# Softmax shares in a latent-attention kernel: GpSimd weights the exponentials of three heads, TensorE spreads the shares of the fourth

## The chip, the cores and the metric

One core of a Trainium2 chip runs the whole kernel. The metric is device time in microseconds, the median of three runs. The engines of a core run their own instruction streams and meet at semaphores: TensorE (PE; its weight loads are listed as PEld), VectorE (DVE), ScalarE (ACT), GpSimd (POOL) and SyncE (SP, which only issues transfers here).

## The reference

One encoder layer over two sequences of 1024 and 512 tokens (1536 together, 12 tiles of 128): RMSNorm, a combined input projection, three mixers side by side (latent attention with 4 heads, centred pooling, gated linear attention), SiLU gates, an output projection, a residual add and a last RMSNorm. The change lies in the attention:

```python
s = (einsum('bqhd,bkhd->bhqk', qn, k_nope) + einsum('bqhr,bkr->bhqk', qr, k_rope))
p = softmax(s * MLA_SCALE, axis=-1)
return einsum('bhqk,bkhd->bqhd', p, v)        # v = latent @ w_v, per head
```

Everything is float32. The softmax is exp(s - max) divided by the row's sum; the inverse of that sum is called the share of a query here. The product with the keys' values is taken in two stages: the probabilities times the latent tokens (128 wide), and that times the head's w_v.

## The kernel before, in words

The program has three phases in order of time: a front phase (norm, input projection, pooling, linear attention; to about 410 us), the attention phase `phase_mla_attend` (about 413 to 632 us), and the output phase. Almost all float32 products are made as three products of split halves (`product`, L76 to L80: hi*hi, hi*lo, lo*hi).

The attention phase runs 48 steps, 12 query tiles for each of 4 heads. `QUERY_TILES` gives for a step the tile and the number of key tiles, `count`: 8 for the first eight tiles of a head (the long sequence: 1024 keys, wide steps) and 4 for the last four (512 keys, narrow steps). Each engine has its own loop over the step number m, and the order inside a step is written out by hand with lags. For step m:

- PE: `scores(m)` into PSUM banks 2*(m%2) and the next; in some steps `project`; in odd steps `values(p)` of the pair of tiles p=(m-4)//2; `turn(m-2)`, which transposes the exponentials of step m-2 tile by tile, in float32 against the identity (L1894); in even steps `output(p)`, p=(m-5)//2.
- DVE: the row maximum (L1821) and from it the bias -max*scale (L1824) of step m; in odd steps the gather of an earlier pair (L1829, L1831) and the low half of the latent product (L1837); the share of step m-2, a reciprocal of `total` (L1843); the low halves of the turned exponentials (L1848).
- ACT: the exponentials of step m with their row sum in `total` (L1763), written to `weights`, a ring of 3 slots; the high halves of the turned exponentials (L1777) and of the latent product (L1791).
- POOL has nothing to do in the first three heads. Its queue holds the split of the output weights `w_out` (L1712, L1717), which waits for their load, and the gates of the first output tile.

The exponentials are transposed and multiplied unnormalised, so the shares come in at the end of each pair of query tiles: a share is one number per partition (query), but the product of `output` has the queries along the free axis. Two transposes of `share[:, i].broadcast_to([P, P])` against the identity (L1914) therefore spread the 2*128 shares over all partitions, into the second half of the PSUM bank of the pair. DVE copies them to `share_row` (L1829), since it takes one operand from PSUM, and multiplies (L1831) into `keep.mixed`.

Waits that matter: `scores(m)` waits for the exponentials of m-2 (`exp_done`); the exponentials of m wait for the transposes of m-3 (`turned`); `turn(m)` waits for `exp_done`; `values(p)` waits for the gather of p-2; `output(p)` waits for `share_ready` and `latent_lo_ready`.

Of the kernel before, what the change touches and what calls it, by code (L numbers as in the profile page):

```python
# [17 lines left out]
ALU = mybir.AluOpType  # L18
# [3 lines left out]
P = 128  # L22
# [3 lines left out]
TILES = NT // P  # L26
# [15 lines left out]
HEADS = 4  # L42
# [1517 lines left out]
SLOTS = 3  # L1560
PAIR = 2 * P
PAIRS = STEPS // 2

TURN_LAG, VALUES_LAG, OUTPUT_LAG, GATHER_LAG = 2, 4, 5, 6
PROJECT_AT = {5: 0, 7: 1, 9: 2}
MIX_GATES_STEP, HEADS_GATES_STEP = STEPS - 6, STEPS - 4
SPLIT_FIRST_STEP = STEPS - 3
# [40 lines left out]
def phase_mla_attend(nc, cx, block, front, rope_dram, gates_dram, mix_dram, w_out_dram, w_out_loaded, gate_loaded, mix_loaded, psum,  # L1608
# [6 lines left out]
    with ExitStack() as mem:  # L1615
# [26 lines left out]
        latent_lo_ready = sem("a_latent_lo_ready")  # L1642
        output_done = sem("a_output_done")
        share_copied = sem("a_share_copied")
        gathered = sem("a_gathered")
        w_hi_set = sem("a_w_hi_set")
        w_split = sem("a_w_split")
# [42 lines left out]
        @block.gpsimd  # L1690
        def _(pool):
            mix, of_heads = keep.mix_first[:, :, :], keep.mixed[:, :, 0:P]
            heads_gates, mix_gates = keep.gate_first[:, 0:4, :], keep.gate_first[:, 4:KT, :]

            def multiply(out, gates):
                return nc.gpsimd.tensor_tensor(out, out, gates, ALU.mult)

            for k in range(KT):
                if k == 6:
                    pool.wait_ge(gate_loaded, 16)  # L1700
                    pool.wait_ge(mix_loaded, 16)
                    multiply(mix, mix_gates).then_inc(first_step, 1)
                if k == 7:
                    pool.wait_ge(gate_turned, 1)
                    nc.gpsimd.tensor_scalar(mix_gates, mix_gates, 1.0, 0.5, ALU.add, ALU.mult).then_inc(first_step, 1)
                    pool.wait_ge(first_step, 2)
                    multiply(mix, mix_gates).then_inc(first_step, 1)
                pool.wait_ge(w_out_loaded[k], 16)
                if k == 5:
                    pool.wait_ge(scores_done, TILES * (HEADS - 1))  # L1710
                for half in range(2):
                    nc.gpsimd.tensor_copy(keep.w_out_hi[k][half][:, :], keep.w_out[k][:, half * BLK:(half + 1) * BLK])\  # L1712
                      .then_inc(w_hi_set, 1)
                for half in range(2):
                    cols = slice(half * BLK, (half + 1) * BLK)
                    pool.wait_ge(w_hi_set, 2 * k + half + 1)
                    nc.gpsimd.tensor_tensor(keep.w_out_lo[k][:, cols], keep.w_out[k][:, cols],  # L1717
                                            keep.w_out_hi[k][half][:, :].bitcast(F32), ALU.subtract).then_inc(w_split, 1)
            pool.wait_ge(gathered, 3 * TILES // 2 + 1)
            multiply(of_heads, heads_gates).then_inc(first_step, 1)  # L1720
            pool.wait_ge(gate_opened, 1)
            nc.gpsimd.tensor_scalar(heads_gates, heads_gates, 1.0, 0.5, ALU.add, ALU.mult).then_inc(first_step, 1)
            pool.wait_ge(first_step, 5)
            multiply(of_heads, heads_gates).then_inc(gated, 2)
# [80 lines left out]
        def _(dve):  # L1805
# [10 lines left out]
            for m in range(STEPS + GATHER_LAG):  # L1816
                if m < STEPS:
# [5 lines left out]
                    dve.wait_ge(top_ready, m + 1)  # L1823
                    nc.vector.tensor_scalar(bias[:, m:m + 1], top[:, m:m + 1], keep.q_scale[:, tile:tile + 1], -1.0,  # L1824
                                            ALU.mult, ALU.mult).then_inc(bias_ready, 1)
                for p in pair_at(m, GATHER_LAG):
                    h, t = p // (2 * TB), (p % (2 * TB)) * PAIR
                    dve.wait_ge(output_done, p + 1)
                    nc.vector.tensor_copy(share_row[:, p % 2, :], psum[:, 6 + p % 2, PAIR:]).then_inc(share_copied, 1)  # L1829
                    dve.wait_ge(share_copied, p + 1)  # L1830
                    nc.vector.tensor_tensor(keep.mixed[:, h, t:t + PAIR], psum[:, 6 + p % 2, :PAIR],  # L1831
                                            share_row[:, p % 2, :], ALU.mult).then_inc(gathered, 1)
                for h, b in projected_at(m):
# [5 lines left out]
                      .then_inc(latent_lo_ready, 1)  # L1839
                if 0 <= m - TURN_LAG < STEPS:  # L1840
                    tile = m - TURN_LAG
                    dve.wait_ge(exp_done, tile + 1)
                    nc.vector.reciprocal(share[:, tile:tile + 1], total[:, tile:tile + 1]).then_inc(share_ready, 1)  # L1843
                    for n, item in turned_banks(tile):
                        dve.wait_ge(turned_hi_ready, item)
                        at = (slice(None), (tile // 2) % 2, slice(4 * n, 4 * n + 4),
# [13 lines left out]
        def _(pe):  # L1860
# [26 lines left out]
                mm.then_inc(scores_done, 1)  # L1887

            def turn(m):
                pe.wait_ge(exp_done, m + 1)  # L1890
                for n, item in turned_banks(m):
                    pe.wait_ge(turned_lo_ready, item - 2)
                    for k in range(4):
# [14 lines left out]

            def output(p):
                h = p // (2 * TB)  # L1910
                pe.wait_ge(share_ready, 2 * p + 2)
                pe.wait_ge(latent_lo_ready, p + 1)
                for n in range(2):
                    nc.tensor.transpose(psum[:, 6 + p % 2, PAIR + n * P:PAIR + (n + 1) * P],  # L1914
                                        share[:, 2 * p + n:2 * p + n + 1].broadcast_to([P, P]), ident[:, :])
                product(nc, psum[:, 6 + p % 2, :PAIR], keep.w_v_hi[:, h * P:(h + 1) * P], keep.w_v_lo[:, h * P:(h + 1) * P],
                        latent_hi[:, p % 2, :], latent_lo[:, p % 2, :]).then_inc(output_done, 1)

# [405 lines left out]
```

## Time and profile before

| | us |
|---|---|
| median of 3 runs (768.06 to 768.74) | 768.07 |
| profiled execution, its own time | 769.48 |
| span of the profile, first to last instruction | 767.7 |
| PE busy over the span | 749.1 (98%) |
| DVE busy | 410.0 (53%) |
| ACT busy | 308.3 (40%) |
| POOL busy | 221.4 (29%) |

The own time holds 1.8 us that lie outside the span. The profiled execution is 1.41 us longer than the median. Matmuls are pipelined: the duration in a matmul's row overlaps its neighbours', so what one costs PE is the distance from its start to the next start.

### The profile page before, as it was taken

To read this page: it belongs to the slowest core of one execution; us is meant where nothing else is said; L and a number is where in the kernel's file an instruction comes from. 1 tells how busy PE (TensorE), PEld (TensorE's weight loads), DVE (VectorE), ACT (ScalarE), POOL (GpSimd) and SP (SyncE) were. 2 spreads that over 40 slices of the span, in tenths; PEclk is the share of its full clock that TensorE was granted. 3 is DMA by queue.
4 is the path that set the end of the run, shared out by engine and by line. 5 is a ranking of instruction groups with operands and counts; after the bars stand their busy time and mean duration, and the time that the engine had idled before them with its cause. 6 is when DMAs were issued, how large, how long until landed. Compare 5 with 4: busy or idle time off the path is not lost.

```text
span 767.7 us, 14603 instructions
## 1 busy us (share of the span) xinstructions
PE 749.1 (98%) x6044; PEld 630.0 (82%) x6044; DVE 410.0 (53%) x733; ACT 308.3 (40%) x533; POOL 221.4 (29%) x261
## 2 busy tenths in 40 slices
PE   6999999999999999999999999999999999999996
PEld 4997867877888888888887888888888987888885
DVE  3662795366557643106164776767667664443332
ACT  5552624513434432232313645555445643323221
POOL 4123214536556631123500000000009904323320
PEclk9899999999999999999999999999999999999999
DMA  7312022001211222430124000000034025654541
GB/s 259 134 60 75 29 67 82 29 3 43 71 68 46 85 86 96 152 96 28 48 110 165 15 16 28 9 21 14 15 91 185 1 74 160 220 183 136 160 150 55
DMA packets 40188, 64.53 MB, mean 84 GB/s; under 512 B 4256, under 2 KB 23104, under 8 KB 40128
## 3 DMA queue, kind: packets, MB, share of 16 engines
q1 hardware_dynamic: 33984, 49.51, 20.0%
q10 hardware_dynamic: 6144, 14.16, 4.8%
q8 instruction: 45, 0.74, 0.4%
q14 instruction: 15, 0.12, 0.0%
HBM read 44.00 MB, written 19.27 MB: 82 GB/s over the span
## 4 chain that ended last, share of the span: by engine, by line
PE 88%; DVE 5%; DMA 2%; ACT 2%; issue 1%; SPq 1%; POOL 1%; DVEq 0%; POOLq 0%; ACTq 0%
PE psum L78 23%; PE psum L80 22%; PE psum L79 22%; PE psum L1894 5%; PE psum L1885 2%; PE psum L1886 2%; PE psum L1280 2%; PE psum L1174 1%; DMA o_gate_second<-gates_scratch 1%; PE psum L1310 1%; PE psum L1335 1%; DMA n_x_in<-in_x_dram 1%; PE psum L1204 1%; PE psum L1235 1%; PE psum L1914 1%
## 5 line engine op out<-in xcount | busy, mean ns | idle before, releaser
L78 PE MATMUL psum<-h_hi,z_w_hi 128*128 128x512 f32 (+1 forms) x480 | 184.8, 385 | 0.0
L80 PE MATMUL psum<-h_hi,z_w_lo 128*128 128x512 f32 (+1 forms) x480 | 177.8, 370 | 0.0
L79 PE MATMUL psum<-h_lo,z_w_hi 128*128 128x512 f32 (+1 forms) x480 | 177.7, 370 | 0.0
L78 PEld LDWEIGHTS psum<-h_hi,z_w_hi 128*128 128x128 f32 x480 | 91.4, 190 | 18.4 <-issue 2.2
L80 PEld LDWEIGHTS psum<-h_hi,z_w_lo 128*128 128x128 f32 x480 | 91.3, 190 | 15.8
L79 PEld LDWEIGHTS psum<-h_lo,z_w_hi 128*128 128x128 f32 x480 | 91.5, 191 | 14.2 <-issue 0.7
L78 PE MATMUL psum<-o_w_hi,o_m_hi 128*128 128x512 f32 x184 | 72.8, 396 | 0.8 <-DVE o_m_lo L2127 0.7
L80 PE MATMUL psum<-o_w_hi,o_m_lo 128*128 128x512 f32 x184 | 72.3, 393 | 0.0
L79 PE MATMUL psum<-o_w_lo,o_m_hi 128*128 128x512 f32 x184 | 72.2, 392 | 0.0
L1763 ACT ACTIVATE a_weights<-psum,a_bias,mla_q_scale 128x1024 f32<-128x1024 f32 (+1 forms) x48 | 51.2, 1066 | 47.2 <-DVE a_bias L1824 47.0
L769 POOL TENSOR_TENSOR z_w_lo<-z_w_raw,z_w_hi 128x1024 fp32r<-128x1024 f32 x17 | 42.1, 2478 | 95.3 <-ACT z_w_hi L473 95.3
L1712 POOL CAST o_w_hi<-o_w_raw 128x512 fp32r<-128x512 f32 x16 | 9.4, 620 | 196.5 <-DMA o_w_raw<-in_w_out_dram 196.5
L1821 DVE TENSOR_REDUCE a_top<-psum 128x1 f32<-128x1024 f32 (+1 forms) x48 | 50.1, 1043 | 27.7 <-PE psum L1886 27.7
L1777 ACT ACTIVATE a_turned_hi<-psum 128x512 fp32r<-128x512 f32 x80 | 44.3, 597 | 33.7 <-PE psum L1894 32.8
L1848 DVE TENSOR_TENSOR a_turned_lo<-psum,a_turned_hi 128x512 fp32r<-128x512 f32 x80 | 51.9, 683 | 2.7 <-ACT a_turned_hi L1777 2.7
L1033 DVE COPY_PREDICATED g_attn<-g_level_mask,psum 128x256 f32<-128x256 int32 x72 | 32.4, 450 | 38.8 <-ACT g_attn L644 36.7
L80 PE MATMUL psum<-a_turned_hi,mla_tokens_lo 128*128 128x256 f32 x160 | 45.3, 283 | 0.0
L79 PE MATMUL psum<-a_turned_lo,mla_tokens_hi 128*128 128x256 f32 x160 | 45.3, 283 | 0.0
L78 PE MATMUL psum<-a_turned_hi,mla_tokens_hi 128*128 128x256 f32 x160 | 45.1, 282 | 0.0
L2138 DVE TENSOR_TENSOR o_y<-psum,o_x_in 128x512 f32<-128x512 f32 x24 | 16.4, 689 | 52.4 <-PE psum L80 52.4
L1894 PE MATMUL psum<-ident,a_weights 128*128 128x128 f32 x320 | 43.6, 275 | 0.0
L486 ACT ACTIVATE z_gate<-psum 128x512 f32<-128x512 f32 x24 | 14.3, 598 | 71.6 <-PE psum L80 71.6
(236 smaller groups left out, 1446.3 us busy)
## 6 DMA issues: line engine op xcount, KB each, us to landing
z_w_raw<-in_w_z_dram SPq DMA_DIRECT2D x17, 512.0 KB, 3.4
n_x_in<-in_x_dram SPq DMA_DIRECT2D x12, 512.0 KB, 4.0
gates_scratch<-z_gate ACTq DMA_DIRECT2D x24, 256.0 KB, 2.0
o_x_in<-in_x_dram SPq DMA_DIRECT2D x12, 512.0 KB, 3.6
out_dram<-o_y ACTq DMA_DIRECT2D x11, 512.0 KB, 3.1
o_w_raw<-in_w_out_dram SPq DMA_DIRECT2D x8, 512.0 KB, 9.3
rope_scratch<-p_rope_split SPq DMA_DIRECT2D x12, 256.0 KB, 2.3
a_q_rope<-rope_scratch SPq DMA_DIRECT2D x48, 64.0 KB, 1.9
```

What stands on the lines that cost most here:

```text
L78: nc.tensor.matmul(out, a_hi, b_hi, start=first, stop=False)
L79: nc.tensor.matmul(out, a_hi, b_lo, start=False, stop=False)
L80: return nc.tensor.matmul(out, a_lo, b_hi, start=False, stop=last)
L769: nc.gpsimd.tensor_tensor(w_lo[:, o % 2, :], raw_of(o)[:, :], w_hi[:, o % 2, :].bitcast(F32), ALU.subtract).then_inc(w_lo_ready, 1)
L1033: nc.vector.copy_predicated(attn[:, t % 2, :, :], level_mask[:, n, :].bitcast(mybir.dt.int32).unsqueeze(1).broadcast_to([P, HEADS, CHUNK]) ...
L1280: mm = nc.tensor.matmul(psum[CHUNK * half:CHUNK * (half + 1), 2 + head, n * CHUNK:(n + 1) * CHUNK], keys, moving, start=True, stop=True, s ...
L1763: nc.scalar.activation(weights[:, m % SLOTS, 0:count * P].rearrange("p (a k) -> p a k", k=BLK), psum[:, banks, :], ACT.Exp, bias=bias[:, m ...
L1777: nc.scalar.activation(turned_hi[:, p % 2, 4 * n:4 * n + 4, (tile % 2) * P:(tile % 2 + 1) * P], psum[:, 4 + item % 2, :].rearrange("p (k q ...
L1821: nc.vector.tensor_reduce(top[:, m:m + 1], psum[:, banks, :], mybir.AxisListType.XY, ALU.max)\
L1848: nc.vector.tensor_tensor(turned_lo[at], psum[:, 4 + item % 2, :].rearrange("p (k q) -> p k q", k=4), turned_hi[at].bitcast(F32), ALU.subt ...
L1894: mm = nc.tensor.transpose(psum[:, 4 + item % 2, k * P:(k + 1) * P], weights[:, m % SLOTS, (4 * n + k) * P:(4 * n + k + 1) * P], ident[:, :])
L2138: nc.vector.tensor_tensor(y[:, s, cols], psum[:, 1 - s + 2 * half, :], x_in[:, s, cols], ALU.add)\
```

## The change

For the 36 steps of heads 0 to 2 (`WEIGHTED_STEPS`), POOL multiplies the exponentials in place by the share (a `tensor_scalar` with one scalar per partition, 128x1024 in wide and 128x512 in narrow steps) and signals the new semaphore `weighted`, for which `turn(m)` waits in place of `exp_done`. These 36 instructions stand ahead of everything else in POOL's queue of this phase. DVE takes the reciprocal of step m-1 right behind the bias of step m, in place of that of step m-2 later in the step. `output` no longer issues its two share transposes for the 18 pairs of these heads and doesn't wait for `share_ready`; DVE's gather of these pairs is one copy from PSUM to `keep.mixed`. Head 3 works as before.

```diff
--- before.py
+++ after.py
@@ -1562,6 +1562,7 @@
 PAIRS = STEPS // 2
 
 TURN_LAG, VALUES_LAG, OUTPUT_LAG, GATHER_LAG = 2, 4, 5, 6
+WEIGHTED_STEPS = TILES * (HEADS - 1)
 PROJECT_AT = {5: 0, 7: 1, 9: 2}
 MIX_GATES_STEP, HEADS_GATES_STEP = STEPS - 6, STEPS - 4
 SPLIT_FIRST_STEP = STEPS - 3
@@ -1642,6 +1643,7 @@
         latent_lo_ready = sem("a_latent_lo_ready")
         output_done = sem("a_output_done")
         share_copied = sem("a_share_copied")
+        weighted = sem("a_weighted")
         gathered = sem("a_gathered")
         w_hi_set = sem("a_w_hi_set")
         w_split = sem("a_w_split")
@@ -1694,6 +1696,12 @@
 
             def multiply(out, gates):
                 return nc.gpsimd.tensor_tensor(out, out, gates, ALU.mult)
+
+            for m in range(WEIGHTED_STEPS):
+                count = QUERY_TILES[m % TILES][2]
+                pool.wait_ge(share_ready, m + 1)
+                nc.gpsimd.tensor_scalar(weights[:, m % SLOTS, 0:count * P], weights[:, m % SLOTS, 0:count * P],
+                                        share[:, m:m + 1], None, ALU.mult).then_inc(weighted, 1)
 
             for k in range(KT):
                 if k == 6:
@@ -1823,11 +1831,17 @@
                     dve.wait_ge(top_ready, m + 1)
                     nc.vector.tensor_scalar(bias[:, m:m + 1], top[:, m:m + 1], keep.q_scale[:, tile:tile + 1], -1.0,
                                             ALU.mult, ALU.mult).then_inc(bias_ready, 1)
+                if 0 < m <= WEIGHTED_STEPS:
+                    dve.wait_ge(exp_done, m)
+                    nc.vector.reciprocal(share[:, m - 1:m], total[:, m - 1:m]).then_inc(share_ready, 1)
                 for p in pair_at(m, GATHER_LAG):
                     h, t = p // (2 * TB), (p % (2 * TB)) * PAIR
                     dve.wait_ge(output_done, p + 1)
+                    if 2 * p < WEIGHTED_STEPS:
+                        nc.vector.tensor_copy(keep.mixed[:, h, t:t + PAIR], psum[:, 6 + p % 2, :PAIR]).then_inc(gathered, 1)
+                        continue
                     nc.vector.tensor_copy(share_row[:, p % 2, :], psum[:, 6 + p % 2, PAIR:]).then_inc(share_copied, 1)
-                    dve.wait_ge(share_copied, p + 1)
+                    dve.wait_ge(share_copied, p - WEIGHTED_STEPS // 2 + 1)
                     nc.vector.tensor_tensor(keep.mixed[:, h, t:t + PAIR], psum[:, 6 + p % 2, :PAIR],
                                             share_row[:, p % 2, :], ALU.mult).then_inc(gathered, 1)
                 for h, b in projected_at(m):
@@ -1839,8 +1853,9 @@
                       .then_inc(latent_lo_ready, 1)
                 if 0 <= m - TURN_LAG < STEPS:
                     tile = m - TURN_LAG
-                    dve.wait_ge(exp_done, tile + 1)
-                    nc.vector.reciprocal(share[:, tile:tile + 1], total[:, tile:tile + 1]).then_inc(share_ready, 1)
+                    if tile >= WEIGHTED_STEPS:
+                        dve.wait_ge(exp_done, tile + 1)
+                        nc.vector.reciprocal(share[:, tile:tile + 1], total[:, tile:tile + 1]).then_inc(share_ready, 1)
                     for n, item in turned_banks(tile):
                         dve.wait_ge(turned_hi_ready, item)
                         at = (slice(None), (tile // 2) % 2, slice(4 * n, 4 * n + 4),
@@ -1887,7 +1902,10 @@
                 mm.then_inc(scores_done, 1)
 
             def turn(m):
-                pe.wait_ge(exp_done, m + 1)
+                if m < WEIGHTED_STEPS:
+                    pe.wait_ge(weighted, m + 1)
+                else:
+                    pe.wait_ge(exp_done, m + 1)
                 for n, item in turned_banks(m):
                     pe.wait_ge(turned_lo_ready, item - 2)
                     for k in range(4):
@@ -1908,11 +1926,12 @@
 
             def output(p):
                 h = p // (2 * TB)
-                pe.wait_ge(share_ready, 2 * p + 2)
                 pe.wait_ge(latent_lo_ready, p + 1)
-                for n in range(2):
-                    nc.tensor.transpose(psum[:, 6 + p % 2, PAIR + n * P:PAIR + (n + 1) * P],
-                                        share[:, 2 * p + n:2 * p + n + 1].broadcast_to([P, P]), ident[:, :])
+                if 2 * p >= WEIGHTED_STEPS:
+                    pe.wait_ge(share_ready, 2 * p + 2)
+                    for n in range(2):
+                        nc.tensor.transpose(psum[:, 6 + p % 2, PAIR + n * P:PAIR + (n + 1) * P],
+                                            share[:, 2 * p + n:2 * p + n + 1].broadcast_to([P, P]), ident[:, :])
                 product(nc, psum[:, 6 + p % 2, :PAIR], keep.w_v_hi[:, h * P:(h + 1) * P], keep.w_v_lo[:, h * P:(h + 1) * P],
                         latent_hi[:, p % 2, :], latent_lo[:, p % 2, :]).then_inc(output_done, 1)
```

## Rows read from the trace of the kernel before

**Rows 1.** Page, part 1: busy us, share of the span, instructions.
```profile
PE 749.1 (98%) x6044; PEld 630.0 (82%) x6044; DVE 410.0 (53%) x733; ACT 308.3 (40%) x533; POOL 221.4 (29%) x261
```

**Rows 2.** Windows: length, busy us of PE, PEld, DVE, ACT, POOL, clock, DMA.
```profile
413.00:422.00 9.00, 8.08 (x39) 6.46 (x39) 4.22 (x6) 2.91 (x6) 0.00 (x0) 1.00 0.11 31
422.00:575.00 153.00, 153.00 (x984) 136.19 (x983) 105.72 (x219) 80.48 (x153) 0.00 (x0) 1.00 0.09 25
575.00:632.00 57.00, 56.85 (x379) 50.94 (x378) 39.44 (x85) 31.19 (x58) 35.32 (x38) 1.00 0.22 84
```

**Rows 3.** Chain that ended last, 422 to 575 us, its shares by line.
```profile
by line: PE psum L78 21.3%; PE psum L79 21.3%; PE psum L80 21.2%; PE psum L1894 17.2%; PE psum L1885 8.4%; PE psum L1886 8.4%; PE psum L1914 2.3%
```

**Rows 4.** Timeline of PE: start us, us, engine, line, op, shape, count.
```profile
465.45 0.38 PE L1914 MATMUL psum<-ident,a_share 128*128 128x128 f32 x2
465.79 0.28 PE L79 MATMUL psum<-a_latent_lo,mla_w_v_hi 128*128 128x256 f32 x1
465.91 0.29 PE L80 MATMUL psum<-a_latent_hi,mla_w_v_lo 128*128 128x256 f32 x1
...
469.73 0.60 PE L1894 MATMUL psum<-ident,a_weights 128*128 128x128 f32 x4
470.40 0.39 PE L79 MATMUL psum<-mla_ckv_lo,a_q_hi 128*128 128x512 f32 x1
470.63 0.39 PE L80 MATMUL psum<-mla_ckv_hi,a_q_lo 128*128 128x512 f32 x1
```

**Rows 5.** Groups of POOL by shape: count, busy us, mean ns of one, idle before.
```profile
L769 POOL TENSOR_TENSOR z_w_lo<-z_w_raw,z_w_hi 128x1024 fp32r<-128x1024 f32 x17 | 42.1, 2478 | 95.3 <-ACT z_w_hi L473 95.3
...
L769 POOL TENSOR_TENSOR z_w_lo<-z_w_raw_second,z_w_hi 128x1024 fp32r<-128x1024 f32 x1 | 3.4, 3412 | 0.1
...
L827 POOL COPY z_window_sums<-z 128x1024 f32<-128x1024 f32 x2 | 2.1, 1042 | 2.7 <-ACT z L511 2.7
...
L827 POOL COPY z_window_sums<-z 128x512 f32<-128x512 f32 x2 | 1.2, 618 | 0.0
L1705 POOL TENSOR_SCALAR o_gate_first<-o_gate_first 128x512 f32<-128x512 f32 x1 | 0.6, 636 | 0.0
```

**Rows 6.** Timeline of all engines: steps 0 and 1, and the bias of step 13.
```profile
418.49 0.19 ACT L1763 ACTIVATION_READ_ACCUMULATOR a_weights<-psum,a_bias,mla_q_scale 128x1 f32 x1
...
419.31 0.21 DVE L1824 TENSOR_SCALAR a_bias<-a_top,mla_q_scale 128x1 f32<-128x1 f32 x1
...
422.60 0.21 DVE L1824 TENSOR_SCALAR a_bias<-a_top,mla_q_scale 128x1 f32<-128x1 f32 x1
...
422.73 0.15 DVE L1843 RECIPROCAL a_share<-a_total 128x1 f32<-128x1 f32 x1
...
469.76 0.21 DVE L1824 TENSOR_SCALAR a_bias<-a_top,mla_q_scale 128x1 f32<-128x1 f32 x1
```

**Rows 7.** Timeline of PE's weight loads: the transposes of steps 0, 1 and 12.
```profile
420.92 1.02 PEld L1894 LDWEIGHTS psum<-ident,a_weights 128*128 128x128 f32 x8
...
424.08 1.03 PEld L1894 LDWEIGHTS psum<-ident,a_weights 128*128 128x128 f32 x8
...
472.25 1.02 PEld L1894 LDWEIGHTS psum<-ident,a_weights 128*128 128x128 f32 x8
```

**Rows 8.** Timeline of all engines: one signal from POOL to ACT.
```profile
609.40 1.31 POOL L1696 TENSOR_TENSOR mla_mixed<-mla_mixed,o_gate_first 128x512 f32<-128x512 f32 x1
...
610.75 0.63 ACT L1736 ACTIVATE o_gate_first<-o_gate_first 128x512 f32<-128x512 f32 x1 [0.48 <-POOL mla_mixed L1696]
```

**Rows 9.** One line's instructions: ns min/median/max, first and last start.
```profile
L1824 DVE TENSOR_SCALAR a_bias<-a_top,mla_q_scale x48: 213/214/217, 417.1 to 618.6; 128x1 f32<-128x1 f32 x48
```

**Rows 10.** Timelines of POOL and of PE: first weight split, first product that needs the splits.
```profile
577.22 1.17 POOL L1712 CAST o_w_hi<-o_w_raw 128x512 fp32r<-128x512 f32 x2 [196.51 <-DMA o_w_raw<-in_w_out_dram]
...
622.26 0.40 PE L78 MATMUL psum<-o_w_hi,o_first_hi 128*128 128x512 f32 x1
```

## The prediction

> **What bounds the kernel now.** I read the page first: PE is busy for 98% of the span and no other engine for more than 53% [rows 1]. An average over stages doesn't say what limits the attention phase, so I went on to the windows of that phase. Its start (413 to 422 us) has about 1 us in which PE is idle. From 422 to 575 us, which is nearly all of the first three heads, PE is busy for 153.00 of 153.00 us at a granted clock of 1.00, the upper level (2.4 GHz); DVE is busy for 106 us, ACT for 80 and POOL for none [rows 2]. A busy PE need not be the cause, so the third view is the chain of waits of the same stretch: it consists of PE lines alone. No step of it goes to DVE, ACT or a transfer, and the share transposes of L1914 hold 2.3% of it [rows 3]. So in these heads an instruction taken from PE shortens the time by what PE spends on it, as long as nothing else becomes late; and the one thing that the change puts in front of PE is POOL's multiplication.
>
> **What goes away on PE.** The duration in a matmul's row (0.27 us for one share transpose) is not its price, since matmuls overlap. The distance of starts is. From the first share transpose of a pair to the second product of `output` it is 465.79 - 465.45 = 0.34 us; a product of 256 columns takes 0.12 us from start to start (465.91 - 465.79), so the two transposes hold 0.22 us, 0.11 each [rows 4]. One could fear that the first product behind a transpose is slow for another reason, and that this stays. Where four transposes are followed by a 512-column product with no share between them, the distance to the second product is 470.40 - 469.73 = 0.67 us = 4 x 0.11 + 0.23, and 0.23 is what such a product takes anyway (470.63 - 470.40) [rows 4]. So there is no such penalty. The chain gives the same by another way: 2.3% of 153 us is 3.5 us over the 16 pairs whose `output` lies in that window, 0.22 us a pair; its rounding (2.25 to 2.35%) makes 0.215 to 0.225 [rows 3]. The change removes the transposes of 18 pairs: 18 x 0.22 = 3.96 us, with 3.87 and 4.05 as ends. Their weight loads and one wait per pair go with them and are in the distances.
>
> **What is added on POOL, and when it has to be done.** No row shows a `tensor_scalar` of 128x1024 with a scalar per partition. From below: the copy of that shape takes 1.04 us [rows 5]. The nearest row is a `tensor_scalar` with constants of 128x512 at 0.64 us, close to the copy of its shape at 0.62; add the copies' difference (1.04 - 0.62) for twice the columns and it is 1.06 us [rows 5]. From above: the two-input subtractions of 128x1024 take 2.48 us, and the dearest of them took 3.41 [rows 5]. One tensor is read, as in the copy, so I take 1.06 us, and keep 1.04 and 3.41 as ends.
>
> The Trainium skill speaks against such work on GpSimd: GPSIMD Engine Reference, section 3.1 (Elementwise — side-by-side cycle accounting), gives about 2.6 cycles per element and section 4.1 sends elementwise work on a tile to VectorE. By that figure a wide multiplication would be 1024 x 2.6 / 1.2 GHz = 2.2 us, an estimate from that page. Section 3.1 ties that figure to two-input work and section 4.1 names about line rate for one input; the trace's copy and two-input rows agree with both.
>
> When must it be done? The reciprocal now stands behind the next step's bias. In the rows a reciprocal starts 0.13 us after the start of the bias in front of it and takes 0.15, so the share is there 0.28 us after that start [rows 6]. A signal from POOL to another engine took 0.04 us (609.40 + 1.31 to 610.75) [rows 8]; I take 0.04 for DVE to POOL and for POOL to PE. With w for the multiplication, the weighted exponentials of step m are there at bias(m+1) + 0.36 + w. They are due when PE loads the first of them for its transposes. Step 0: 420.92 - 419.31 = 1.61 us, so w may be 1.25. Step 1: 424.08 - 422.60 = 1.48, so w may be 1.12; step 2 is like step 1 within 0.01. Step 12: 472.25 - 469.76 = 2.49, so w may be 2.13; step 24 is like it [rows 6, 7]. Gone through in the same way, the other 31 steps allow more than 2.7. The first three steps are tight because no `values` stands between their scores and their transposes; steps 12 and 24 because the `values` and the transposes in between are those of narrow tiles.
>
> With w = 1.06 nothing waits: the tightest step keeps 0.06 us. For w = 1.25, a wide step at twice the narrow row, steps 1 and 2 wait 0.13 us once. I put 0.1 us down for this. For larger w the stalls are 2w - 2.38 us in the first three steps together (the delay of step 0 moves the scores and the bias of step 3, behind which the share of step 2 is made; that of step 1 doesn't), plus 2(w - 2.13) in steps 12 and 24 from w = 2.13, and from about 2.8 on something in other steps, which I leave out.
>
> **What is moved, and what stays hidden.** On PE, `output` and the next step's scores stand behind the wait in `turn`; they are late by the stalls just given and by nothing else. On DVE, the earlier reciprocal now waits for the exponentials of m-1 ahead of the gather and the low halves. In step 1, the tightest, that wait is over at 418.49 + 0.19 = 418.68, ahead of the bias at 419.31 [rows 6]. The share's copy and multiplication become one copy, so DVE gets back one instruction a pair; it had 47 us idle in the 153 [rows 2], and nothing in the chain waits for it [rows 3], so I count zero. POOL working beside DVE could slow it: the bias took 213 to 217 ns in all 48 steps, also in head 3 where POOL is busy for 35 of 57 us [rows 2, 9], so zero. POOL's queue: the split of `w_out`, which began at 577.22 when its load landed [rows 10], now stands behind the 36th multiplication, that of step 35, and may begin later. The splits ended before POOL's next instruction at 609.40 and are needed at 622.26 [rows 8, 10]: 12.9 us of cover, and only what is late beyond these would cost. SP's transfers wait for the same events as before and move with them.
>
> **The sum.** Against the profiled execution's own time: 769.48 - 3.96 + 0.1 = 765.6 us. That execution is 1.41 us over the median of the runs; taken off, 764.2 us, 0.5% faster.
>
> **The rivals.**
> 1. POOL's multiplication costs as much as a two-input one, 2.48 us. Then the first three steps stall 2 x 2.48 - 2.38 = 2.58 us and steps 12 and 24 together 0.70, 3.28 in all, and 0.7 us is left: 767.4, no difference that can be told. For: no row has a scalar per partition, and POOL's rows differ fourfold for other operations. Against: copy and `tensor_scalar` of 128x512 are equal within 3%. The skill's page named above has the rule for this rival, with its 2.2 us.
> 2. Slower. POOL's multiplication takes 3.41 us, as its dearest row of this size. The stalls are 2 x 3.41 - 2.38 = 4.44 us in the first three steps and 2 x 1.28 = 2.56 in steps 12 and 24, 7.0 at least, so 768.07 - 3.96 + 7.0 = 771.1. From w = 2.65 the stalls (4w - 6.64) eat the whole gain, and from 3.02 the kernel is slower by more than 0.2%. For: it is POOL's own time, once, in this trace. Against: once in 18, and for two inputs.
> 3. The change does nothing: something other than PE sets the pace of the heads, and PE's 0.22 us a pair become idle time; 768.1. For: ACT and DVE work in turns with PE in every step. Against: PE has no idle time at all in 153 us, and the chain has no other engine [rows 2, 3].
>
> **How the numbers follow.** 0.2% of the time, 1.5 us, is about what a measurement of this kernel can tell from no change. The forecast (w up to 1.3, 764.0 to 764.5) has a chance of 0.72; a w between 1.3 and 2.26, where 1.5 us or more of the gain is left (up to 766.5), 0.12; rival 1 with its surroundings 0.08, rival 3 0.03, rival 2 0.05. So faster 0.84, no difference 0.11, slower 0.05. The low end is the largest gain (4.05 us, no stall: 764.0) less 0.3 for the runs' own spread; the high end is the edge of the second case: 763.7 to 766.5.
>
> **What would show it right or wrong.** Right: L1914 has 12 instructions instead of 48; the new POOL line has 24 wide ones near 1.06 us and 12 narrow near 0.64; PE is again busy without a gap from 422 us on, and the transposes of steps 0 to 2 wait for POOL by 0.1 us at most; a head takes 6 x 0.22 = 1.3 us less. Wrong: waits of PE for POOL in steps 0 to 2, 12 and 24 (then w is over 2.1); longer DVE rows beside POOL's; gaps of PE in the middle of a head; or `w_out` splits that end close to their first product.

## The result and the profile after

The change made the kernel slower, by about as little as can be told from no change: 770.17 us (median of 20 runs) against 769.05 for the kernel before beside it, a ratio of 1.0018 with a 95% interval of 1.001 to 1.0027, so 0.8 to 2.1 us. The forecast was 3.9 us less.

The profiled execution after took 771.27 us, its span is 769.5. The page's part 1 answers to [rows 1]: PE has less to do, as intended, and POOL 87 us more.

```profile
PE 746.5 (97%) x6008; PEld 625.8 (81%) x6008; DVE 402.9 (52%) x715; ACT 307.7 (40%) x533; POOL 308.4 (40%) x297
```

The windows by stage, to be held against [rows 2] (columns as there). Of the 153 us from 422 to 575, where PE had no idle time before, it now idles for 2.95, and before 422 for 0.7 us more than it did:

```profile
413.00:422.00 9.00, 7.36 (x30) 5.47 (x30) 4.03 (x7) 3.11 (x5) 2.04 (x1) 1.00 0.13 37
422.00:575.00 153.00, 150.05 (x950) 132.16 (x951) 98.45 (x201) 79.46 (x151) 83.52 (x35) 1.00 0.08 21
575.00:632.00 57.00, 56.94 (x380) 51.00 (x379) 38.90 (x83) 31.81 (x59) 36.89 (x39) 1.00 0.23 88
```

The chain of the same stretch answers to [rows 3]. The 2.3% of the share transposes are gone, and POOL's multiplication has come into it with 7.5%:

```profile
by line: PE psum L78 19.5%; PE psum L80 19.5%; PE psum L79 19.5%; PE psum L1912 17.0%; PE psum L1901 7.5%; PE psum L1900 7.5%; POOL a_weights L1703 7.5%; DVE a_top L1829 2.4%; DVE a_bias L1832 0.4%; issue 0.4%; DVE a_share L1836 0.2%
```

The reason stands in the groups of POOL by shape. A wide multiplication took 2.85 us and a narrow one 1.57, where the forecast had 1.06 and 0.64:

```profile
L1703 POOL TENSOR_SCALAR a_weights<-a_weights,a_share 128x1024 f32<-128x1024 f32 x24 | 68.4, 2849 | 82.1 <-DVE a_share L1836 82.1
L1703 POOL TENSOR_SCALAR a_weights<-a_weights,a_share 128x512 f32<-128x512 f32 x12 | 18.8, 1568 | 27.9 <-DVE a_share L1836 27.9
```

PE's weight loads that waited for POOL, from the timeline (answers to [rows 7]; in brackets the idle time and what ended it). These seven are all: the transposes of steps 0 to 2, 12, 14, 24 and 26. Five of them the forecast had named as the tightest; steps 14 and 26 it had not (see e4_covered):

```profile
422.86 0.86 PEld L1912 LDWEIGHTS psum<-ident,a_weights 128*128 128x128 f32 x8 [1.71 <-POOL a_weights L1703]
426.16 0.86 PEld L1912 LDWEIGHTS psum<-ident,a_weights 128*128 128x128 f32 x8 [0.32 <-POOL a_weights L1703]
430.83 0.85 PEld L1912 LDWEIGHTS psum<-ident,a_weights 128*128 128x128 f32 x8 [1.70 <-POOL a_weights L1703]
...
475.65 0.86 PEld L1912 LDWEIGHTS psum<-ident,a_weights 128*128 128x128 f32 x8 [0.83 <-POOL a_weights L1703]
483.97 0.86 PEld L1912 LDWEIGHTS psum<-ident,a_weights 128*128 128x128 f32 x8 [0.39 <-POOL a_weights L1703]
...
529.10 0.86 PEld L1912 LDWEIGHTS psum<-ident,a_weights 128*128 128x128 f32 x8 [0.83 <-POOL a_weights L1703]
...
537.43 0.85 PEld L1912 LDWEIGHTS psum<-ident,a_weights 128*128 128x128 f32 x8 [0.39 <-POOL a_weights L1703]
```

For the experiments a finer measure than the whole time is wanted, since the stretch in front of the attention phase alone differs by 1.5 us between profiles (411.95 to 413.48 us). I use the distance from the first product of the scores to the first product of the output weights, from here on the phase for short. In the kernel before these rows of PE's timeline are the first below and the one in [rows 10]: 622.26 - 413.19 = 209.07 us.

```profile
413.19 0.47 PE L78 MATMUL psum<-mla_ckv_hi,a_q_hi 128*128 128x512 f32 x1 [0.65 <-DMA a_q_rope<-rope_scratch]
```

After the change it is 623.09 - 413.48 = 209.61 us, 0.54 more:

```profile
413.48 0.47 PE L78 MATMUL psum<-mla_ckv_hi,a_q_hi 128*128 128x512 f32 x1 [0.60 <-DMA a_q_rope<-rope_scratch]
...
623.09 0.40 PE L78 MATMUL psum<-o_w_hi,o_first_hi 128*128 128x512 f32 x1
```

### The profile page after: what moved, and what is told of

It reads as the page before. It is cut to its first block, busy times and chain, and to the rows that moved or that the text cites. A ratio compares the mean times of both kernels' runs of the same rounds, so it can differ in the third digit from the quotient of the medians.

```text
span 769.5 us, 14531 instructions
## 1 busy us (share of the span) xinstructions
PE 746.5 (97%) x6008; PEld 625.8 (81%) x6008; DVE 402.9 (52%) x715; ACT 307.7 (40%) x533; POOL 308.4 (40%) x297
## 4 chain that ended last, share of the span: by engine, by line
PE 87%; DVE 5%; DMA 2%; POOL 2%; ACT 2%; issue 1%; SPq 1%; DVEq 0%; POOLq 0%; ACTq 0%
PE psum L78 23%; PE psum L80 22%; PE psum L79 22%; PE psum L1912 5%; PE psum L1280 2%; PE psum L1901 2%; PE psum L1900 2%; POOL a_weights L1703 1%; PE psum L1174 1%; PE psum L1310 1%; PE psum L1335 1%; DMA n_x_in<-in_x_dram 1%; DMA o_gate_second<-gates_scratch 1%; PE psum L1204 1%; PE psum L1235 1%
## 5 line engine op out<-in xcount | busy, mean ns | idle before, releaser
L1703 POOL TENSOR_SCALAR a_weights<-a_weights,a_share 128x1024 f32<-128x1024 f32 (+1 forms) x36 | 87.1, 2422 | 110.0 <-DVE a_share L1836 110.0
L1912 PEld LDWEIGHTS psum<-ident,a_weights 128*128 128x128 f32 x320 | 35.6, 140 | 10.7 <-POOL a_weights L1703 6.2
```

Source lines behind the costliest of these rows:

```text
L1703: nc.gpsimd.tensor_scalar(weights[:, m % SLOTS, 0:count * P], weights[:, m % SLOTS, 0:count * P], share[:, m:m + 1], None, ALU.mult).then_ ...
L1912: mm = nc.tensor.transpose(psum[:, 4 + item % 2, k * P:(k + 1) * P], weights[:, m % SLOTS, (4 * n + k) * P:(4 * n + k + 1) * P], ident[:, :])
```

## The experiments

Ten kernels ran; all times are against the kernel before on the same chip. The column of times is the phase of the profiled execution, with its two starts in brackets.

| kernel | phase, us (first score, first product) | ratio to before (95%) |
|---|---|---|
| before | 209.07 (413.19, 622.26) | |
| after | 209.61 (413.48, 623.09) | 1.0018 (1.001 to 1.0027) |
| e1_none | 204.96 (413.15, 618.11) | 0.9961 (0.9948 to 0.9974) |
| e2_const | 209.17 (412.36, 621.53) | 1.0006 (0.9997 to 1.0016) |
| e3_dve | 207.04 (413.39, 620.43) | 0.9983 (0.9973 to 0.9993) |
| e4_covered | 205.95 (411.95, 617.90) | 0.9955 (0.9942 to 0.9967) |
| e5_forms | 209.03 (412.31, 621.34) | one run, no interval |
| e6_two_ops | 205.00 (412.05, 617.05) | 0.9949 (0.9933 to 0.9965) |
| e7_mixed | 205.74 (412.45, 618.19) | 0.9959 (0.9944 to 0.9973) |
| e8_stalls | 213.37 (412.36, 625.73) | 1.005 (1.0037 to 1.0064) |
| e9_two_inputs | 206.15 (412.67, 618.82) | 0.9959 (0.9943 to 0.9976) |
| e10_again | 209.59 (412.21, 621.80) | 1.0012 (1.0 to 1.0024) |

### e1_none: the saving alone

```diff
-            for m in range(WEIGHTED_STEPS):
-                count = QUERY_TILES[m % TILES][2]
-                pool.wait_ge(share_ready, m + 1)
-                nc.gpsimd.tensor_scalar(...).then_inc(weighted, 1)
...
-                if m < WEIGHTED_STEPS:
-                    pe.wait_ge(weighted, m + 1)
-                else:
-                    pe.wait_ge(exp_done, m + 1)
+                pe.wait_ge(exp_done, m + 1)
```

> The changed kernel without GpSimd's multiplications: the first three heads leave out the division by the softmax sum, the share transposes of their 18 pairs are gone, the transposes of the exponentials wait for the exponentials again. Theory (the price of the multiplication alone was mis-sized, the rest of the sum holds): no wait of TensorE for GpSimd, 3.9 to 4.0 us less than the kernel before, and about 5 us less than the changed kernel. Rival 1 (the transposes were not on the path): within 1 us of the kernel before. Rival 2 (the output phase is what became longer, by its transfers meeting other work): less than 3 us gained, with the tail behind the first product of the output weights longer than the 145.4 us of before.

The phase is 4.11 us shorter than before's; PE has no idle time from 422 to 575 us. So the share transposes were on the path, at 4.11 / 18 = 0.228 us a pair, and rival 1 of this run falls. Rival 2 falls too: from the first product of the output weights to the end it was 763.7 - 618.11 = 145.6 us, as before (145.4). The whole time fell by 0.39%, 3.0 us; its interval, 2.0 to 4.0 us, ends just short of the phase's 4.1.

### e2_const: the same instruction without the share

```diff
-                                        share[:, m:m + 1], None, ALU.mult).then_inc(weighted, 1)
+                                        1.0, None, ALU.mult).then_inc(weighted, 1)
```

> The changed kernel with the constant 1.0 in place of the share as GpSimd's factor: same instruction count, places, waits and bytes, but no scalar per partition; the division by the softmax sum is left out in three heads. Theory (the scalar read from SBUF makes the instruction dear): a wide one takes 1.06 us and a narrow one 0.64, TensorE waits 0.1 us at most, 3.9 us less than the kernel before. Rival (size, working in place, or sharing SBUF with the other engines makes it dear): a wide one still takes 2.85 us and a narrow one 1.57, and the time is that of the changed kernel, 1 us over the kernel before.

The theory fell. With a constant, POOL's groups show hardly less:

```profile
L1703 POOL TENSOR_SCALAR a_weights<-a_weights 128x1024 f32<-128x1024 f32 x24 | 66.5, 2773 | 83.4 <-DVE a_share L1836 83.4
```

The scalar read per partition costs 2.85 - 2.77 = 0.08 us, and the phase stayed near the changed kernel's (209.17 against 209.61), as the rival has it. So something else separates this instruction from the `tensor_scalar` of [rows 5], which took 0.64 us for half the columns.

### e3_dve: the multiplication on VectorE

```diff
                     nc.vector.reciprocal(share[:, m - 1:m], total[:, m - 1:m]).then_inc(share_ready, 1)
+                    at = (slice(None), (m - 1) % SLOTS, slice(0, QUERY_TILES[(m - 1) % TILES][2] * P))
+                    dve.wait_ge(share_ready, m)
+                    nc.vector.tensor_scalar(weights[at], weights[at], share[:, m - 1:m], None, ALU.mult).then_inc(weighted, 1)
```

(The loop on GpSimd is taken out.)

> VectorE makes the 36 multiplications in place of GpSimd, right behind each reciprocal; the result is the reference's. VectorE's price for 128x1024 from SBUF is not in the trace; its 128x512 with a scalar per partition from PSUM took 0.75 us, its maximum over 128x1024 1.22 us, so 0.6 to 1.4 us. Theory (only the multiplication's price lost the gain): TensorE waits under 0.5 us in all and the kernel is 3 to 4 us faster than before. Rival (a multiplication between exponentials and transposes costs the gain on any engine, since it makes the low halves behind it late): TensorE waits in the middle of the heads, 0 to 2 us gained.

DVE took 0.754 us for a wide one, and no weight load of PE waited for the weighted exponentials. The gain was half of the expected, 2.0 us in the phase. So the rival holds for this engine: DVE's low halves of the turned exponentials stand behind its multiplication, and PE waited for them. PE's weight loads that waited for low halves by the profile (total, times, longest) are those of four projections, the first in step 5, the others in step 9 of each head:

```profile
PEld psum L78 <- DVE a_turned_lo L1860: 2.0, 4, 0.6
...
431.39 0.19 PEld L78 LDWEIGHTS psum<-mla_cq_hi,mla_w_q_hi 128*128 128x128 f32 x1 [0.30 <-DVE a_turned_lo L1860]
...
451.61 0.19 PEld L78 LDWEIGHTS psum<-mla_cq_hi,mla_w_q_hi 128*128 128x128 f32 x1 [0.58 <-DVE a_turned_lo L1860]
```

That is not all. From the first score to the scores of step 6 it is 436.56 - 413.39 = 23.17 us here and 435.62 - 413.15 = 22.47 in e1_none, so 0.70 of the 2.08 us lost against e1_none are lost in the first steps. There the loads of the transposes of steps 1 and 2, which by the code wait for low halves as well, have 0.35 us of idle time in front of them, for which the profile names no releaser. Nearly all of the rest is lost behind the three projections in step 9.

### e4_covered: only where there is time for 2.85 us

```diff
+SPREAD_PAIRS = (0, 1, 6, 12)
+def by_pool(p):
+    return 2 * p < WEIGHTED_STEPS and p not in SPREAD_PAIRS
...
-            for m in range(WEIGHTED_STEPS):
+            for m in [n for n in range(WEIGHTED_STEPS) if by_pool(n // 2)]:
```

(`turn`, `output` and the gather ask `by_pool` in place of the step's number.)

> GpSimd weights only the pairs whose transposes leave time for 2.85 us; pairs 0, 1, 6 and 12 (steps 0 to 3, 12, 13, 24, 25) keep their share transposes. The result is the reference's. Theory (stalls only where the slack is under 2.85 us): 14 pairs times 0.22 us, 3.1 us less than the kernel before, with steps 14 and 26 waiting under 0.1 us each. Rival (GpSimd's work costs TensorE time elsewhere too, or in the output phase): less than 2 us gained.

3.12 us less in the phase, and 0.45% (3.5 us) in the time. Two weight loads wait for POOL, 0.4 us each where under 0.1 was expected, in steps 14 and 26; PE itself shows no gap. Most of these waits are not the change's: in the kernel before the same load already had 0.27 us of idle time in front of it (the first row below; the second is this run's), so about 0.1 is new.

```profile
480.83 0.96 PEld L1894 LDWEIGHTS psum<-ident,a_weights 128*128 128x128 f32 x8 [0.27 <-issue]
...
479.09 0.86 PEld L1928 LDWEIGHTS psum<-ident,a_weights 128*128 128x128 f32 x8 [0.40 <-POOL a_weights L1719]
```

So with POOL's instruction as dear as it is, the place decides: the multiplications of 14 pairs cost next to nothing, and those of the other four turn 3.1 us gained into 0.5 lost.

### e5_forms: the price of one instruction by itself

```diff
+            pool.wait_ge(scores_done, TILES + 1)
+            nc.gpsimd.memset(v, 0.5)
+            nc.gpsimd.tensor_scalar(v, v, 1.0, None, ALU.mult)                 # L1706
+            nc.gpsimd.tensor_scalar(v, v, 1.0, 1.0, ALU.mult, ALU.mult)        # L1708
+            nc.gpsimd.tensor_scalar(v, v, one, None, ALU.mult)                 # L1710
+            nc.gpsimd.tensor_scalar(v, v, one, 1.0, ALU.mult, ALU.mult)        # L1712
+            nc.gpsimd.tensor_scalar(v, v, 0.0, 1.0, ALU.add, ALU.mult)         # L1714
+            nc.gpsimd.tensor_scalar(v, v, 0.0, None, ALU.add)                  # L1716
+            nc.gpsimd.tensor_scalar(v4, v4, 1.0, None, ALU.mult)               # L1718
+            nc.gpsimd.tensor_scalar(u, v, 1.0, None, ALU.mult)                 # L1720
+            nc.gpsimd.tensor_copy(u, v)                                        # L1722
+            nc.gpsimd.tensor_tensor(v, v, one.broadcast_to([P, D_MODEL]), ALU.mult)  # L1724
```

(In the kernel before; each waits for the one in front; `one` is a column of scalars, `v4` the tile as eight runs of 128, `u` another tile. Three more forms and a second round are left out here.)

> The kernel before, with a row of trial instructions added on GpSimd, which is idle in these heads: from step 13 on it runs 14 forms on a tile of its own, twice, each waiting for the one in front. The output is the reference's. It measures one instruction's price by itself, with 0.5 as data. The 128x1024 in-place multiplication by a constant took 2.77 us on the exponentials, the 128x512 form with two operations (add, then multiply) 0.64 us on the gates. Theory A (an instruction with one operation and the second left out takes a slow path): one operation 2.8 us, two operations 1.1 us, whatever is multiplied. Theory B (multiply is slow as the first operation, add is not): 2.8 us for both multiplications, 1.1 us for both additions. Theory C (the exponentials' data, or the other engines' work on that tile, make it slow): every form 1.1 us here. Theory D (the shape: one run of 1024 against four of 128): 1.1 us for the form written as eight runs of 128 and 2.8 for the flat one. A multiplication by a broadcast column takes 2.5 us as two-input work in all of them.

The timeline of POOL:

```profile
465.38 2.78 POOL L1706 TENSOR_SCALAR a_trial<-a_trial 128x1024 f32<-128x1024 f32 x1
468.24 1.05 POOL L1708 TENSOR_SCALAR a_trial<-a_trial 128x1024 f32<-128x1024 f32 x1
469.39 2.85 POOL L1710 TENSOR_SCALAR a_trial<-a_trial,mla_q_scale 128x1024 f32<-128x1024 f32 x1
472.34 1.14 POOL L1712 TENSOR_SCALAR a_trial<-a_trial,mla_q_scale 128x1024 f32<-128x1024 f32 x1
473.56 1.05 POOL L1714 TENSOR_SCALAR a_trial<-a_trial 128x1024 f32<-128x1024 f32 x1
474.70 2.79 POOL L1716 TENSOR_SCALAR a_trial<-a_trial 128x1024 f32<-128x1024 f32 x1
477.57 2.78 POOL L1718 TENSOR_SCALAR a_trial<-a_trial 128x1024 f32<-128x1024 f32 x1
480.43 2.78 POOL L1720 TENSOR_SCALAR a_trial_other<-a_trial 128x1024 f32<-128x1024 f32 x1
483.27 1.04 POOL L1722 COPY a_trial_other<-a_trial 128x1024 f32<-128x1024 f32 x1
484.39 1.89 POOL L1724 TENSOR_TENSOR a_trial<-a_trial,mla_q_scale 128x1024 f32<-128x1024 f32 x1
```

Theory A holds and B, C and D fall. One operation takes 2.78 us whether it multiplies (L1706) or adds (L1716), in runs of 128 (L1718) or into another tile (L1720), on data of one value. Two operations take 1.05 us (L1708, L1714), with the scalars from SBUF 1.14 (L1712). The row on which the forecast's price rests, L1705 in [rows 5], has two operations, an add and a multiply; the new instruction has one. The row's name, TENSOR_SCALAR, is the same for both. One expectation was missed: the multiplication by a broadcast column (L1724) took 1.89 us, not the 2.5 of two-input work.

### e6_two_ops: the change with a second operation

```diff
-                                        share[:, m:m + 1], None, ALU.mult).then_inc(weighted, 1)
+                                        share[:, m:m + 1], 1.0, ALU.mult, ALU.mult).then_inc(weighted, 1)
```

> The changed kernel with a second operation in GpSimd's instruction: times the share, then times 1.0. The result is the reference's. Theory A (one operation alone takes a slow path): a wide one takes 1.1 to 1.2 us, TensorE waits 0.2 us at most, and the attention phase comes to 205.1 us from its first score to the first product of the output weights, 4 us less than before. Theories B, C, D: 2.85 us or more, 0.5 us more than before in the phase.

As theory A has it: 205.00 us for the phase, 4.07 less than before, and 0.51% in the time (765.22 us against 769.30). Of the versions that keep the division by the softmax sum, this has the shortest phase; e3_dve, e4_covered, e7_mixed and e9_two_inputs beat both kernels too, by less in the phase. POOL's groups, and the window from 422 to 575 us:

```profile
L1703 POOL TENSOR_SCALAR a_weights<-a_weights,a_share 128x1024 f32<-128x1024 f32 x24 | 27.2, 1131 | 115.4 <-DVE a_share L1836 115.4
L1703 POOL TENSOR_SCALAR a_weights<-a_weights,a_share 128x512 f32<-128x512 f32 x12 | 8.3, 695 | 40.8 <-DVE a_share L1836 40.8
...
422.00:575.00 153.00, 153.00 (x974) 135.91 (x973) 100.41 (x204) 82.02 (x156) 37.85 (x40) 1.00 0.12 37
```

PE has no gap and nothing of it waits for POOL. The tight steps are just met, as the timeline shows. In step 0 the multiplication ends at 418.56 + 1.13 = 419.69 and the first weight load is at 419.77; in step 1, one of the two tightest by the forecast, they are at 421.84 + 1.14 = 422.98 and 423.03.

```profile
418.17 0.21 DVE L1832 TENSOR_SCALAR a_bias<-a_top,mla_q_scale 128x1 f32<-128x1 f32 x1
418.30 0.15 DVE L1836 RECIPROCAL a_share<-a_total 128x1 f32<-128x1 f32 x1
...
418.56 1.13 POOL L1703 TENSOR_SCALAR a_weights<-a_weights,a_share 128x1024 f32<-128x1024 f32 x1 [38.93 <-DVE a_share L1836]
419.77 0.81 PEld L1912 LDWEIGHTS psum<-ident,a_weights 128*128 128x128 f32 x6
...
421.84 1.14 POOL L1703 TENSOR_SCALAR a_weights<-a_weights,a_share 128x1024 f32<-128x1024 f32 x1 [2.16 <-DVE a_share L1836]
423.03 0.93 PEld L1912 LDWEIGHTS psum<-ident,a_weights 128*128 128x128 f32 x8
```

### e7_mixed: VectorE where POOL has no time

```diff
+VECTOR_PAIRS = (0, 1, 6, 12)
...
+                    if by_vector(m - 1):
+                        dve.wait_ge(share_ready, m)
+                        nc.vector.tensor_scalar(weights[at], weights[at], share[:, m - 1:m], None, ALU.mult).then_inc(weighted_first, 1)
```

> The changed kernel with VectorE in place of GpSimd for the eight steps of pairs 0, 1, 6 and 12, which have less cover than 2.85 us; GpSimd weights the other 28. The result is the reference's. Theory (a wide multiplication takes 0.75 us on VectorE, and eight of them fit): all 18 share transposes are gone and nothing waits, 205.1 us for the attention phase, 0.9 us less than with 14 pairs on GpSimd alone. Rival (VectorE's low halves come late in these steps too, as where it did all 36): 0.2 us of waits for VectorE per such pair, which gives back the 0.9 us.

205.74 us, 0.2 less than with 14 pairs where 0.9 was expected. The 0.7 that is missing is lost in the first steps, as in e3_dve: from the first score to the scores of step 6 it is 435.61 - 412.45 = 23.16 us here and 434.52 - 412.05 = 22.47 in e6_two_ops, 0.69 more, and at the end of the phase it is 0.74 more. The loads of the transposes of steps 1 and 2 and of the projection in step 5 are late:

```profile
423.64 0.95 PEld L1925 LDWEIGHTS psum<-ident,a_weights 128*128 128x128 f32 x8 [0.35 <-issue]
427.08 0.95 PEld L1925 LDWEIGHTS psum<-ident,a_weights 128*128 128x128 f32 x8 [0.37 <-issue]
430.45 0.19 PEld L78 LDWEIGHTS psum<-mla_cq_hi,mla_w_q_hi 128*128 128x128 f32 x1 [0.30 <-DVE a_turned_lo L1874]
```

So the rival holds for pairs 0 and 1. Pairs 6 and 12, and the two waits for POOL in steps 14 and 26 (0.4 us each), cost the phase next to nothing.

### e8_stalls: GpSimd's part alone

```diff
-                    if 2 * p < WEIGHTED_STEPS:
-                        nc.vector.tensor_copy(keep.mixed[:, h, t:t + PAIR], psum[:, 6 + p % 2, :PAIR]).then_inc(gathered, 1)
-                        continue
...
-                if 2 * p >= WEIGHTED_STEPS:
-                    pe.wait_ge(share_ready, 2 * p + 2)
+                pe.wait_ge(share_ready, 2 * p + 2)
```

> The changed kernel with the share transposes, their copy and the multiplication by the shares back in all pairs: the shares are then applied twice in three heads. It shows GpSimd's part of the change alone, without the part that saves. Theory (the two parts add up): the kernel before plus the stalls, 4.5 us by the difference of the two parts, so 213.6 us for the attention phase against 209.07 before, and 0.6% in the time. Rival (what is saved on TensorE and what it waits hide each other in part): under 3 us more than before.

213.37 us, 4.30 more than before, 0.50% in the time. The parts nearly add up: -4.11 + 4.30 = +0.19 us, against +0.54 for both together. The rival, that they hide each other, falls: together they cost 0.35 us more than their sum. Where these 0.35 us arise is not shown.

### e9_two_inputs: a price in between

```diff
-                nc.gpsimd.tensor_scalar(weights[:, m % SLOTS, 0:count * P], weights[:, m % SLOTS, 0:count * P],
-                                        share[:, m:m + 1], None, ALU.mult).then_inc(weighted, 1)
+                nc.gpsimd.tensor_tensor(weights[:, m % SLOTS, 0:count * P], weights[:, m % SLOTS, 0:count * P],
+                                        share[:, m:m + 1].broadcast_to([P, count * P]), ALU.mult).then_inc(weighted, 1)
```

> The changed kernel with GpSimd's multiplication written as two-input work, the share broadcast along the row; the result is the reference's. By itself that form took 1.89 us for 128x1024. It lies between the two prices tried so far (1.13 and 2.85 us) and so tests the stall formula of the prediction at a third point. Theory (the first three steps stall 2w - 2.38 us in all, steps 12 and 24 only from 2.13): 1.4 us of stalls in steps 0 to 2, none in 12 and 24, so 209.07 - 4.1 + 1.4 = 206.4 us for the attention phase, 0.35% less time than before. Rival (the stall is a step: late or not late): the 209.6 us of the changed kernel, or the 205.0 of the form with two operations.

206.15 us where 206.4 was expected; 0.41% less time than before. The stalls cost 206.15 - 204.96 = 1.19 us against e1_none, where the formula has 1.4. They are neither nothing nor those of the changed kernel, so the rival falls. The waits are in the steps of the formula, three at the start and none in steps 12 and 24:

```profile
421.05 0.86 PEld L1912 LDWEIGHTS psum<-ident,a_weights 128*128 128x128 f32 x8 [0.74 <-POOL a_weights L1703]
424.34 0.85 PEld L1912 LDWEIGHTS psum<-ident,a_weights 128*128 128x128 f32 x8 [0.33 <-POOL a_weights L1703]
428.07 0.86 PEld L1912 LDWEIGHTS psum<-ident,a_weights 128*128 128x128 f32 x8 [0.76 <-POOL a_weights L1703]
```

### e10_again: what lies outside the attention phase

No edit; the changed kernel.

> The changed kernel once more, beside the kernel before on the same chip. Its profile was 0.54 us longer than before's in the attention phase, 0.29 in front of it and 1.0 behind it. Theory (only the attention phase is the change's, what lies outside scatters from execution to execution): 209.6 us again for the phase, another number in front and behind, and a ratio of 1.0005 to 1.002. Rival (the change also lengthens the output phase): again about 1 us more behind the phase than before's 128.7 us from the first to the last product there.

The phase repeats to 0.02 us, and the ratio is 1.0012. But the rival has something too: from the first product of the second output tile to the last product of all it was 129.60 us, as in the first profile (762.74 - 633.08 = 129.66) and not as in the kernel before (760.97 - 632.27 = 128.70; 128.69 in e5_forms, the same program there). The difference is one wait in the output phase, for the third tile. PE's timeline before:

```profile
650.17 0.49 PE L78 MATMUL psum<-o_w_hi,o_m_hi 128*128 128x512 f32 x1 [0.68 <-DVE o_m_lo L2127]
```

and after:

```profile
651.93 0.50 PE L78 MATMUL psum<-o_w_hi,o_m_hi 128*128 128x512 f32 x1 [1.59 <-DVE o_m_lo L2146]
```

ACT's queue opens the fourth tile's gates (`o_gate_second`) ahead of the third tile's high half, and waits for their load: from issue to ACT's use it took 644.99 - 640.06 = 4.93 us before and 646.77 - 640.94 = 5.83 after. The wait was 1.44 us in e10_again and 1.63 in e6_two_ops, 0.85 in e2_const and 0.61 in e8_stalls, which both keep POOL's dear multiplication. So it is not tied to the stalls, and why the load takes longer in some of these programs stays open.

## Why the prediction was wrong

**The step that failed** is the price of POOL's multiplication: "The nearest row is a `tensor_scalar` with constants of 128x512 at 0.64 us, close to the copy of its shape at 0.62 [...] so I take 1.06 us". It measured 2.85 us. The row was of an instruction with two operations, and the new one has one; e5_forms shows that this alone makes 2.78 us of 1.05, and e6_two_ops that with the price corrected the rest of the sum comes out. The code showed the two operations (`ALU.add, ALU.mult` at L1705); I compared shape and name only. The bounds did hold it, 1.04 to 3.41, but by luck, since the upper one is of two-input work; I took the value at the low end and gave the stretch above 2.26 a chance of 0.13.

**The saving** was right: 3.96 us were forecast for 18 pairs, e1_none measured 4.11.

**The deadlines and the stalls** were right to about 0.2 us, and the forecast's own formula gives the outcome once the price is put in. For w = 2.85 the first three steps stall 2 x 2.85 - 2.38 = 3.32 us; from the first score to the load of step 2's transposes it is 430.83 - 413.48 = 17.35 us after and was 427.26 - 413.19 = 14.07 before (row below), 3.28 more. Steps 12 and 24 were to stall 0.72 us each; their loads waited 0.83. Together the formula has 4w - 6.64 = 4.76 us, and the phase shows 209.61 - 204.96 = 4.65 between the changed kernel and e1_none. The net would have been +0.8 us; the phase has +0.54. For w = 1.89 the first three steps were to stall 1.40; e9_two_inputs has 428.07 - 412.67 - 14.07 = 1.33 up to that load, and 1.19 over the whole phase. For w = 1.13 nothing was to wait but a few hundredths; in e6_two_ops the load of step 1 comes 423.03 - 412.05 = 10.98 us after the first score, 0.09 later than before (424.08 - 413.19 = 10.89), and PE has no gap.

```profile
427.26 1.02 PEld L1894 LDWEIGHTS psum<-ident,a_weights 128*128 128x128 f32 x8
```

**What was counted at nothing** held: DVE's rows beside POOL are the same (the bias 214 ns in the median, as in [rows 9]), the copy in the gather costs no time on the path, and the output weights' splits were not late, since POOL still waited for their load (0.4 us).

**Rivals.** Rivals 1 and 2 were the right mechanism, a dear multiplication whose stalls eat the gain, with prices on either side of the measured one; the result lies between them, as w = 2.85 lies between 2.48 and 3.41. What makes it dear, the single operation, neither of them named. Rival 3 fell with e1_none. The estimate of 2.2 us from the Trainium skill (GPSIMD Engine Reference, section 3.1) was nearer than my row, though for another reason: it is for two-input work, which took 2.48 us in [rows 5] and 1.89 with a broadcast column. That one-input work runs at about line rate (the Trainium skill, GPSIMD Engine Reference, section 4.1) agrees with the trace of e5_forms for a copy and for two operations, 1.04 and 1.05 us for 1024 columns, and not for one operation, 2.78.

**What is left over.** The phase explains 0.54 us of the 0.8 to 2.1. The wait in the output phase is 0.8 to 0.9 us longer in both profiles of the changed kernel. It would make up the rest (0.54 + 0.96 = 1.5), but that is argued from two profiles, and why the load takes longer is not shown.

## What to carry to other kernels

A row is a price only for the same instruction: compare the operands and the number of operations in the code, not the name and shape that the profile gives. Where no row has the form, give its bounds the chances that they deserve, or choose a form that has a row. And before work is put between two engines, list the deadline of every step: 31 of 36 had time for 2.7 us and more, the three at the start and the two behind narrow tiles had not and decided the result, and leaving their pairs out (e4_covered) already gained 3.1 of the 4.1 us. An engine that is fast enough can still lose the gain through its own later work: VectorE's multiplication took 0.754 us and made its low halves late (e3_dve).

## What the runs showed of the hardware that was not expected

On GpSimd a `tensor_scalar` with one operation on 128x1024 float32 with a constant takes 2.78 us and one with two operations 1.05 (e5_forms); there adding "times 1.0" makes it 2.6 times faster. Why one operation is slower is not shown. A scalar per partition in place of a constant adds 0.07 to 0.09 us. From the narrow and the wide rows of the changed kernel, (2.849 - 1.568) / 512 = 2.5 ns a column for one operation; with two, (1.131 - 0.695) / 512 = 0.85 ns. A two-input multiplication whose second input is a broadcast column takes 1.89 us (e5_forms, e9_two_inputs), less than the one with a single operation. VectorE does the same work from SBUF in 0.754 us (e3_dve).
